# Output projection: three column groups token-major, turned back in 32-blocks by VectorE

## What is computed

```python
mixed = jnp.concatenate([a_out, r_out], axis=-1)      # 256 x 2048
x = x + jnp.einsum('bse,ed->bsd', mixed, w_out)       # w_out 2048 x 2048
h = rms_norm(x, ffn_norm[0])
u = jnp.einsum('bsd,df->bsf', h, w_up[0])             # and so on
```

## Time and profile before

| | us |
|---|---|
| median of 3 runs | 1949.3 (1949.26 to 1949.41) |
| the profiled execution | 1950.1 |
| its span | 1948.0 |
| TensorE busy | 1932.6 |
| VectorE busy | 1393.2 |
| ScalarE busy | 1112.2 |
| output projection, first matmul to first matmul of the up projection | 349.71 to 438.75 |

### The profile page before, as it was taken

One profiled execution on the slowest core, in us unless ns is written; L12 is line 12 of the kernel. 1 busy time (PEld: TensorE's weight loads), 2 busy tenths in 40 slices (PEclk: granted clock), 3 DMA queues, 4 the chain that ended last, 5 costly groups with the idle time before them and its releaser, 6 DMA issues.

```text
span 1948.0 us, 31302 instructions
## 1 busy us (share of the span) xinstructions
PE 1932.6 (99%) x11078; PEld 1688.6 (87%) x11078; DVE 1393.2 (72%) x2152; ACT 1112.2 (57%) x1845; POOL 48.7 (3%) x53
## 2 busy tenths in 40 slices
PE   8999999999999999999999999999999999999998
PEld 8888888888888888888888888888888888888887
DVE  6667786767777777777655557877777777755555
ACT  6555544656665666665555456666665566545554
POOL 0002240000000000000000000000000000000000
PEclk9999999999999999999999999999999999999999
DMA  9555555555555555555565555555555555555653
GB/s 324 196 171 160 185 165 164 194 187 182 194 194 185 184 191 194 189 184 167 194 216 185 185 170 182 186 194 190 183 188 193 194 184 184 192 179 184 205 189 108
DMA packets 205202, 364.91 MB, mean 187 GB/s; under 512 B 6563, under 2 KB 49100, under 8 KB 205132
## 3 DMA queue, kind: packets, MB, share of 16 engines
q1 hardware_dynamic: 203388, 362.34, 56.0%
q10 hardware_dynamic: 1744, 1.63, 0.3%
HBM read 361.83 MB, written 2.11 MB: 187 GB/s over the span
## 4 chain that ended last, share of the span: by engine, by line
PE 98%; DVE 1%; ACT 0%; DMA 0%; issue 0%; DVEq 0%; SPq 0%
PE ps L389 53%; PE ps L393 26%; PE ps L462 7%; PE ps L466 3%; PE ps L496 2%; PE ps L499 2%; PE ps L498 2%; PE ps L480 0%; PE ps L483 0%; PE ps L482 0%; DVE ssq L1249 0%; DVE lo L1119 0%; PE ps L668 0%; PE ps L670 0%; PE ps L528 0%; PE ps L595 0%
## 5 line engine op out<-in xcount | busy, mean ns | idle before, releaser
L745 ACT ACTIVATE hi<-raw 128x512 fp32r<-128x512 f32 x1352 | 844.8, 630 | 799.6 <-PE ps L393 650.6
L1119 DVE TENSOR_TENSOR lo<-raw,hi 128x512 fp32r<-128x512 f32 x1360 | 927.9, 697 | 511.6 <-ACT hi L745 506.8
L389 PE MATMUL ps<-h,hi 128*128 128x512 f32 x2816 | 958.1, 394 | 0.0
L393 PE MATMUL ps<-h,lo 128*128 128x256 f32 x2816 | 733.7, 277 | 0.0
L389 PEld LDWEIGHTS ps<-h,hi 128*128 128x128 f32 x2816 | 507.8, 188 | 97.8 <-DVE lo L1119 0.2
L393 PEld LDWEIGHTS ps<-h,lo 128*128 128x128 f32 x2816 | 528.7, 188 | 25.6
L389 PE MATMUL ps<-act,hi 128*128 128x512 f32 x1392 | 480.6, 394 | 0.0
L393 PE MATMUL ps<-act,lo 128*128 128x256 f32 x1392 | 380.4, 277 | 0.0
L389 PEld LDWEIGHTS ps<-act,hi 128*128 128x128 f32 x1392 | 258.7, 188 | 57.8
L393 PEld LDWEIGHTS ps<-act,lo 128*128 128x128 f32 x1392 | 261.3, 188 | 2.8
L462 PE MATMUL ps<-h,hi 128*128 128x512 f32 x576 | 183.2, 399 | 0.0
(11 more groups left out here) (183 smaller groups left out, 1120.2 us busy)
## 6 DMA issues: line engine op xcount, KB each, us to landing
raw<-in_w_up SPq DMA_DIRECT2D x176, 1024.0 KB, 5.0
raw<-in_w_down SPq DMA_DIRECT2D x88, 1024.0 KB, 5.1
raw<-in_w_in SPq DMA_DIRECT2D x54, 1024.0 KB, 5.1
raw<-in_w_out SPq DMA_DIRECT2D x16, 1024.0 KB, 5.1
raw<-in_pool_w SPq DMA_DIRECT2D x4, 1024.0 KB, 5.3
raw<-in_w_in SPq DMA_DIRECT2D x8, 256.0 KB, 4.8
x<-in_xT SPq DMA_DIRECT2D x8, 128.0 KB, 4.6
x<-in_xT SPq DMA_DIRECT2D x2, 512.0 KB, 7.7
```

Of the source, the lines that this page charges most:

```text
L389: pe.matmul(ps[:, bank + m, :], hi[:, kt, m * P:(m + 1) * P], mv, start=first and kt == 0, stop=False, skip_group_check=True)
L393: return pe.matmul(ps[:, bank + m, S:2 * S], lo[:, kt, m * P:(m + 1) * P], mv[:, 0:S], start=False, stop=last and kt == KT - 1, skip_group ...
L745: a_.activation(hi[:, kt, :], raw[:, slot, kt, :], ACT.Copy).then_inc(hi_done, 1)
L1119: ve.tensor_tensor(lo[:, kt, :], raw[:, slot, kt, :], hi[:, kt, :].bitcast(F32), ALU.subtract).then_inc(lo_done, 1)
```

## The change

Groups 0 to 2 of the output projection run in token_unit, with mixed as the stationary operand (its new argument src); group 3 stays in wide_unit. Their sums stand token-major in two banks of PSUM. turn_mixed transposes them in blocks of 32 x 32: 16 steps a group, each reads 32 tokens (partitions) and, of each token tile and each of four feature tiles, 32 features, and writes them to 32 partitions of qb[0], 256 elements per partition. Two steps stand behind each lo of the units n % 4 = 1 and 2 of the next group. add_turned_mixed then waits for the last of them and adds qb[0] to x in one operation, after unit n % 4 = 2. So the high half of h and the squares move from n % 4 = 1 to n % 4 = 3 on ScalarE; h_lo moves from n % 4 = 2 to n % 4 = 0 of the group after (n = 8 and 12) and, for group 2, to up unit 0; add_squares moves behind unit 12 and, for group 2, behind add_mixed(3) in up unit 0. The x_half semaphore now counts one addition of this stage in place of four.

```diff
@@ -110,6 +110,7 @@
 
     scratch = nc.dram_tensor("bias_strip", (BD, SPAN), F32, kind="Internal").ap()
 
+    TURN = 32
     NEAR = P + max(POOL_WINDOWS)
 
     ctx = ExitStack()
@@ -236,6 +237,7 @@
         mix_hi = sem("mix_hi")
         mix_lo = sem("mix_lo")
         x_half = sem("x_half")
+        m_turned = sem("m_turned")
         half_in = sem("half_in")
         half_sum = sem("half_sum")
         sum_a = sem("sum_a")
@@ -484,15 +486,15 @@
                                        skip_group_check=True)
                     mm.then_inc(w_used, 1)
 
-            def token_unit(n, acc, first, last, j, ready=None):
+            def token_unit(n, acc, first, last, j, ready=None, src=h):
 
                 for kt in range(KT):
                     pe.wait_ge(lo_done, KT * n + kt + 1)
                     if ready is not None:
                         ready(kt)
                     for t in range(2):
-                        xh = h[:, KT * j + kt, t * P:(t + 1) * P]
-                        xl = h[:, KT * j + kt, S + t * P:S + (t + 1) * P]
+                        xh = src[:, KT * j + kt, t * P:(t + 1) * P]
+                        xl = src[:, KT * j + kt, S + t * P:S + (t + 1) * P]
                         pe.matmul(acc[:, t, :], xh, hi[:, kt, :], start=first and kt == 0, stop=False,
                                   skip_group_check=True)
                         pe.matmul(acc[:, t, :], xh, lo[:, kt, :], start=False, stop=False, skip_group_check=True)
@@ -651,8 +653,12 @@
                 for j in range(4):
                     def mixed_tile(kt, j=j):
                         pe.wait_ge(mix_lo, (KT * j + kt) // 2 + 1)
-                    wide_unit(U_OUT + 4 * g + j, 0, wide_bank(G), j == 0, j == 3, lambda kt: mixed[:, KT * j + kt, :],
-                              mixed_tile if g == 0 else None, opening(j) if g else None)
+                    if g < 3:
+                        token_unit(U_OUT + 4 * g + j, ps[:, wide_bank(G):wide_bank(G) + 2, :], j == 0, j == 3, j,
+                                   mixed_tile if g == 0 else None, mixed)
+                    else:
+                        wide_unit(U_OUT + 4 * g + j, 0, wide_bank(G), j == 0, j == 3, lambda kt: mixed[:, KT * j + kt, :],
+                                  None, opening(j))
 
             for l in range(DEPTH):
                 if l == 1:
@@ -907,7 +913,7 @@
                     head_root(6, 8)
             for n in range(16):
                 g = n // 4 - 1
-                spread = n >= 4 and n % 4 == 1
+                spread = n >= 4 and n % 4 == 3
                 w_hi(U_OUT + n, 0, n % 4, 16 * (R_OUT[0] + n // 4 + 1),
                      h_spread(g, 1, G_OUT + g + 1) if spread else None)
                 if n == 0:
@@ -1288,12 +1294,26 @@
                 ve.tensor_tensor(sc[:, 0, 0:S], ps[:, 4, 0:S], dec[:, r, :], ALU.mult).then_inc(decayed, 1)
                 ve.tensor_tensor(sc[:, 0, S:S + P], ps[:, 4, S:S + P], dec[:, r, 0:P], ALU.mult).then_inc(decayed, 1)
 
+            def turn_mixed(g, step):
+
+                ve.wait_ge(w_used, KT * (U_OUT + 4 * (g + 1)))
+                b, tok, feat = wide_bank(G_OUT + g), step // 4 * TURN, step % 4 * TURN
+                rows = ps[tok:tok + TURN, b:b + 2, :].rearrange("p t (m f) -> p t m f", m=4)[:, :, :, feat:feat + TURN]
+                cols = qb[0][feat:feat + TURN, :, :].rearrange("p m (t s) -> p t m s", t=2)[:, :, :, tok:tok + TURN]
+                ve.transpose(cols, rows).then_inc(m_turned, 1)
+
+            def add_turned_mixed(g):
+
+                xs = x[:, 4 * g:4 * g + 4, :]
+                ve.wait_ge(m_turned, 16 * (g + 1))
+                ve.tensor_tensor(xs, qb[0][:, :, :], xs, ALU.add).then_inc(evacuated, 1)
+
             def add_mixed(g):
 
                 ve.wait_ge(w_used, KT * (U_OUT + 4 * (g + 1)))
                 b, xs = wide_bank(G_OUT + g), x[:, 4 * g:4 * g + 4, :]
                 ve.tensor_tensor(xs, ps[:, b:b + 4, 0:S], xs, ALU.add).then_inc(x_half, 1)
-                ve.wait_ge(x_half, g + 1)
+                ve.wait_ge(x_half, 1)
                 ve.tensor_tensor(xs, ps[:, b:b + 4, S:2 * S], xs, ALU.add).then_inc(evacuated, 1)
 
             ve.memset(ones[:, :], 1.0).then_inc(setup, 1)
@@ -1364,12 +1384,23 @@
                 if n == 55:
                     mix_ret(4)
                     norm_ret(7)
+            def beside_out(n):
+
+                def between(kt):
+                    if n in (8, 12):
+                        h_lo_group(1, n // 4 - 2, 1, [kt])
+                    if n >= 4 and n % 4 in (1, 2):
+                        for step in range(2):
+                            turn_mixed(n // 4 - 1, 8 * (n % 4 - 1) + 2 * kt + step)
+                return between
+
             for n in range(16):
                 g = n // 4 - 1
-                spread = n >= 4 and n % 4 == 2
-                w_lo(U_OUT + n, 0, n % 4, between=(lambda kt: h_lo_group(1, g, 1, [kt])) if spread else None)
-                if g >= 1 and n % 4 == 3:
-                    add_squares(1, g)
+                w_lo(U_OUT + n, 0, n % 4, between=beside_out(n))
+                if n == 12:
+                    add_squares(1, 1)
+                if n >= 4 and n % 4 == 2:
+                    add_turned_mixed(g)
                 if n == 0:
                     take_out(len(ACCS) - 1)
                     mixed_lo(4)
@@ -1381,8 +1412,6 @@
                     mixed_lo(6)
                     mix_ret(7)
                     mixed_lo(7)
-                if n >= 4 and n % 4 == 0:
-                    add_mixed(n // 4 - 1)
 
             def up_add(q, Gp):
 
@@ -1431,7 +1460,7 @@
                 ve.wait_ge(w_used, KT * (U_DN[l] + DN_UNITS * (g + 1)))
                 b, xs = wide_bank(G_DN[l] + g), x[:, 4 * g:4 * g + 4, :]
                 ve.tensor_tensor(xs, ps[:, b:b + 4, 0:S], xs, ALU.add).then_inc(x_half, 1)
-                ve.wait_ge(x_half, 4 * (l + 1) + g + 1)
+                ve.wait_ge(x_half, 1 + 4 * l + g + 1)
                 ve.tensor_tensor(xs, ps[:, b:b + 4, S:2 * S], xs, ALU.add).then_inc(evacuated, 1)
 
             for l in range(DEPTH):
@@ -1460,14 +1489,15 @@
                     q = i * 2 + (l * 2 * PAIRS - 1)
                     for j in range(UP_UNITS):
                         between = None
-                        if peel and l == 0 and j == 2:
-                            between = lambda kt: h_lo_group(1, 3, 1, [kt])
+                        if peel and l == 0 and j in (0, 2):
+                            between = lambda kt: h_lo_group(1, 2 if j == 0 else 3, 1, [kt])
                         if peel and l == 1:
                             between = lambda kt: h_lo_group(3, j, 3, [kt])
                         w_lo(U_UP[l] + j, i * (8 * KT), j, between=between)
                         if peel:
                             if l == 0 and j == 0:
                                 add_mixed(3)
+                                add_squares(1, 2)
                             if l == 0 and j == 3:
                                 add_squares(1, 3)
                             if l == 1 and j == 0:
@@ -1554,7 +1584,7 @@
                 b, xs = wide_bank(G_DN[1] + 3) + m, x[:, 12 + m, :]
                 ve.wait_ge(tail_mm, m + 1)
                 ve.tensor_tensor(xs, ps[:, b, 0:S], xs, ALU.add).then_inc(x_half, 1)
-                ve.wait_ge(x_half, 8 + 3 + m + 1)
+                ve.wait_ge(x_half, 5 + 3 + m + 1)
                 ve.tensor_tensor(xs, ps[:, b, S:2 * S], xs, ALU.add).then_inc(last_added, 1)
             ve.wait_ge(token_rms, 1)
             ve.reciprocal(rms[:, 2:4], rms[:, 0:2]).then_inc(token_rstd, 1)
```

## The result

The changed kernel takes 1953.9 us (median, 1953.45 to 1954.4) against 1949.5 (1949.2 to 1950.14) in 13 runs each: 4.4 us more, a ratio of 1.0022 with a 95% interval from 1.0015 to 1.0029. The forecast was 1954.3, slower by 5.0 us. The profiled execution has a span of 1952.3 us against 1948.0.

The account below looks back on a forecast made before the run. TensorE's matmul stream bounds the kernel, lost time coming only where it waits for its feeding ring. Stalls 3.9 + 0.3 + 1.2 + 1.0 = 6.4 us, less 1.4, give +5.0: 1954.3 us; range 1948.2 to 1962.

Parts of the forecast that it names:

- Gain of the form: Output projection, groups 0 to 2: token-major matmuls at the pooling projection's rate shorten TensorE's stream by 1.4 us.
- Price of a turn: VectorE, each 32-partition transpose: 0.48 us start to start, held until the last operation ends because partitions change.
- rival (b): VectorE's turns cost 0.40 to 0.455 us each; stalls 1.5 to 5 us, 1949.5 to 1953.1, taken as 1951.5 us; chance 0.25.
- the filling of a block: VectorE, each turn: a 32-column block must fill before it can drain, adding 0.03 us.
- Allowed lag, 2.46 us: VectorE may fall 2.46 us behind before TensorE stalls; 3.75 behind at n % 4 = 3 gives a 1.3 us stall.
- Second group: TensorE's stall beside the second group's turns: 1.3 us as in each group, plus 0.3 us for a carried remainder.
- The 0.3 us that was carried in: Units 8 and 12 regain only 0.35 us a step, so earlier lag goes on and costs 0.3 us.
- Third group: TensorE's stall beside the third group's turns: 1.3 us as in each group, plus 1.2 us with add_squares in unit 12.
- First up unit: h_lo, add_mixed(3) and add_squares meet on VectorE: 3.2 us behind, 2.54 allowed, 0.3 carried in; 1.0 us of stall.
- Everything at no cost: Later h, PSUM banks, constant x_half waits and ScalarE's block at n % 4 = 3 were all to cost nothing.
- The sign named for it: Profile after: TensorE and its loads wait for lo some 6 us, longest at units 7, 11, 15 and second up unit.
- Rival (a): VectorE's turns overlap, 0.33 to 0.36 us each; only the first up unit stalls, 0.6 to 0.7: 1948.6 us; chance 0.16.

Follow-up runs that it names:

- no_turn: Changed kernel without its 48 turns, the addition taking whatever the buffer holds: -0.93 us against the kernel before (ratio 0.9996).
- t_same: Changed kernel with all turns reading partitions 0 to 31 and writing partitions 0 to 31: -0.59 us against the kernel before (ratio 0.9997).
- t_read: Changed kernel with turns writing partitions 0 to 31 only, those read changing at each turn: +1.5 us against the kernel before, single run.
- t_write: Changed kernel with turns reading partitions 0 to 31 only, those written changing at each turn: +2.4 us against the kernel before, single run.
- order: Changed kernel's new VectorE and ScalarE order alone, all four groups wide, no turns: +0.41 us against the kernel before (ratio 1.0002).
- c_cross: Changed kernel with a plain copy in place of each transpose, same partitions: +3.04 us against the kernel before (ratio 1.0015).

## Why the prediction was right

The mechanism and the places held, and the sum was 5.0 us for 4.4 measured. Luck had a part in how near that is: the stalls come to 5.4 us (1.27 + 1.36 + 2.04 + 0.69, below) where 6.4 were forecast, every one of the four at or under its forecast, and 0.4 us of the measured loss lies outside the stretch that the sum is about.

- **Gain of the form.** Forecast 1.4 us. In the changed kernel, leaving out the stalls, the groups are 0.53, 0.49 and 0.38 us shorter: 1.40; in no_turn the stage is 1.48 shorter.
- **Price of a turn.** Forecast 0.48 us start to start, held to the end of the last operation; measured 446 ns recorded and 0.47 from start to start, the step 1.67 for 1.68. That is 0.02 above the 0.455 under which the prediction gave the case to rival (b), so the choice was narrow. The reason given (changed partitions) was a guess as far as the rows of before went, and t_same, t_read and t_write bear it out. A part of the 0.48 was right for a wrong reason: the filling of a block was put at 30 ns, but a transpose has 8 ns over a copy on fixed partitions; the rest comes with the changed partitions.
- **Allowed lag, 2.46 us.** The first lo of unit 7 is 14.45 - 8 x 1.36 = 3.6 us behind (forecast 3.75), and TensorE loses 1.38 - 0.23 = 1.15 us there and 0.12 more at the start after it: 1.27 for 1.3.
- **Second group.** 1.36 us, forecast 1.6. The 0.3 us that was carried in was wrong: VectorE's rows

```profile
397.08 0.69 DVE L1125 TENSOR_TENSOR lo<-raw,hi 128x512 fp32r<-128x512 f32 x1
...
421.16 0.68 DVE L1125 TENSOR_TENSOR lo<-raw,hi 128x512 fp32r<-128x512 f32 x1
...
443.08 0.69 DVE L1125 TENSOR_TENSOR lo<-raw,hi 128x512 fp32r<-128x512 f32 x1
```

  have the lo of unit 9 at 397.08, 0.06 us behind its natural place (0.87 after a step that started at 396.15). ScalarE's four h tiles and squares had been made up by then.
- **Third group.** 24.24 - 22.20 = 2.04 us, forecast 2.5. The pile of add_squares was there, 0.93 us in place of 1.2 (lo at 421.16; one step of 1.39 and 0.87 after the group's start at 417.97 would be 420.23). Another term was mis-sized: I set eight steps of 1.68 against 1.36 in each of the three groups, but beside this one TensorE runs group 3, which is wide, 1.39 a step and 2.54 allowed. That is 8 x 0.03 + 0.08 = 0.3 us too much.
- **First up unit.** 6.26 against 5.57 us, 0.69, forecast 1.0. Again no lag was carried in: the last lo of the unit, at 443.08, is 0.87 behind the step that started at 442.21.
- **Everything at no cost.** order shows that the later h costs nothing (stage 89.02 for 89.04). ScalarE did block as foretold, three times and 8.1 us in all, the first time for 2.42 us up to 388.60. No run lengthens this block without the lag, so that it costs nothing is read from the changed kernel alone: TensorE has no wait between the one at 389.22 and the next group's at 412.39.

```profile
388.60 0.51 ACT L757 ACTIVATE h<-x,gains 128x256 fp32r<-128x256 f32 x1 [2.42 <-DVE x L1309]
```

The sign named for it, waits of TensorE and its loads of some 6 us, came as 4.2 us for TensorE and 5.7 for its loads (the two lists overlap), the 0.5 us from before among the 4.2.

The sum with the measured terms: 1.27 + 1.36 + 2.04 + 0.69 - 1.40 = 3.96 us, which is the shift of the first start in the second up unit (448.47 - 349.90 = 98.57 us, before 94.61); it has to close, because gain and stalls are read from the same starts. The span shows 4.3 and the medians 4.4; the rest lies ahead of and behind this stretch and isn't explained further (the stage starts 0.19 later, in code that didn't change).

Rival (a), overlapping turns, is what t_same shows: -0.59 us for a forecast of -0.7. c_cross is rival (b), with 0.45 a turn: +3.0 us, near the upper end of its 1949.5 to 1953.1.

## What to carry to other kernels

Beside a ring in which another engine prepares the next step, an inserted piece is free as long as the lag stays under the ring's allowance; what went beyond it was paid in full here (1.15 us of idle time for a lag of 3.6 against 2.46), and 0.12 us more at the restart. So sum the lag step by step, with the one-off pieces on top, before looking at busy shares. Spread the insertions to the places where the engine waits, as many per step as its idle time there takes. Price VectorE operations that hop between blocks of 32 partitions by recorded length plus 0.03 us (0.446 recorded, 0.47 from start to start here), not by the distance of starts seen on full-width work.

## What the runs showed of the hardware that was not expected

- A change of the 32 partitions lengthens the record too, not only the distance: a transpose of 32 x 256 float32 from PSUM took 412 ns on fixed partitions, 439 to 444 with one side changing at each turn, and 446 in the changed kernel, where the partitions written change at each turn and those read at every fourth; a copy 404 and 421 in the same places. The lo shows a difference too: 0.64 us where it starts ahead of the end of the turn in front of it (375.23 in t_read), 0.68 or 0.69 elsewhere.
- On fixed partitions the transpose of float32 costs nearly what a copy costs: 8 ns more for 256 elements per partition (412 against 404).
- A matmul that restarts behind a wait of 1 us has its successor 0.34 us on (389.22 to 389.56; the same at 412.39) in place of 0.227, so such a stall costs some 0.12 us beyond its idle time.
